# One stored copy of the second block's features, split into parts in the gating-value stage

## The reference, cut to what matters

```python
h = rms_norm(x, pre_norm_w)
proj = h @ w_in                       # 1024 x 7168
hy_in, hy_gate, sg_u, sg_v, sg_gate = jnp.split(proj, [...], axis=-1)
vf = sg_v.astype(jnp.float32).reshape(B, L, N_HEADS_B, HEAD_DIM_B)   # 8 heads of 128
mu = jnp.mean(vf, axis=-1, keepdims=True)
var = jnp.mean(jnp.square(vf - mu), axis=-1, keepdims=True)
vn = (vf - mu) * lax.rsqrt(var + EPS) ...                            # the gating values
```

## Time and profile before

| | |
|---|---|
| median of 3 runs | 3382.54 us (3378.78 to 3385.64) |
| the profiled execution | 3384.93 us, its span 3383.1 us |
| mean granted clock of TensorE | 0.966 of full speed |
| PE busy | 3130.7 us (93%) |
| DVE busy | 2474.3 us (73%) |
| ACT busy | 784.7 us (23%) |
| POOL busy | 296.9 us (9%) |
| DMA | 404.76 MB, mean 120 GB/s |

### The profile page before, as it was taken

One profiled execution on the slowest core, in us unless ns is written; L12 is line 12 of the kernel. 1 busy time (PEld: TensorE's weight loads), 2 busy tenths in 40 slices (PEclk: granted clock), 3 DMA queues, 4 the chain that ended last, 5 costly groups with the idle time before them and its releaser, 6 DMA issues. The chain is left out here.

```text
span 3383.1 us, 32779 instructions
## 1 busy us (share of the span) xinstructions
PE 3130.7 (93%) x12882; PEld 2193.2 (65%) x12882; DVE 2474.3 (73%) x2632; ACT 784.7 (23%) x1354; POOL 296.9 (9%) x420
## 2 busy tenths in 40 slices
PE   6999999888995898999999999999898989889999
PEld 4444445554443687787788888787565656677887
DVE  6989997795883585999999999975556667552221
ACT  2000000683331221000011111112352725431110
POOL 3221220001220350000000000000000000000000
PEclk9999999999997899999999999999999999979999
DMA  6555550202447543665644454421211120334221
GB/s 199 143 141 151 142 154 15 106 1 91 159 155 259 202 131 112 177 167 151 178 139 137 133 145 135 143 75 38 106 53 50 53 100 13 137 111 143 91 91 56
DMA packets 210474, 404.76 MB, mean 120 GB/s; under 512 B 20608, under 2 KB 132416, under 8 KB 202512
## 3 DMA queue, kind: packets, MB, share of 16 engines
q1 hardware_dynamic: 190416, 331.86, 31.4%
q0 software_dynamic: 18752, 62.42, 7.2%
q10 hardware_dynamic: 1152, 8.39, 0.6%
HBM read 316.60 MB, written 86.00 MB: 119 GB/s over the span
## 5 line engine op out<-in xcount | busy, mean ns | idle before, releaser
L1567 PE MATMUL PS<-HH,WH 128*128 128x512 f32 x1536 | 607.6, 396 | 34.6 <-DVE WL L1464 15.4
L1568 PE MATMUL PS<-HL,WH 128*128 128x512 f32 x1536 | 604.6, 394 | 0.0
L1569 PE MATMUL PS<-HH,WL 128*128 128x512 f32 x1536 | 601.8, 392 | 0.0
L741 PE MATMUL PS<-M 128*128 128x512 f32 x1152 | 499.7, 596 | 9.5 <-DVE M L578 7.0
L741 PEld LDWEIGHTS PS<-M 128*128 128x128 f32 x1152 | 219.6, 191 | 289.0 <-issue 278.8
L1567 PEld LDWEIGHTS PS<-HH,WH 128*128 128x128 f32 x1536 | 290.2, 189 | 104.6 <-DVE MB L1501 14.1
L1569 PEld LDWEIGHTS PS<-HH,WL 128*128 128x128 f32 x1536 | 290.2, 189 | 65.3
L1568 PEld LDWEIGHTS PS<-HL,WH 128*128 128x128 f32 x1536 | 290.5, 189 | 61.0
L100 DVE SCALAR_TENSOR_TENSOR HP<-MF,HP 128x1024 f32<-128x1024 f32 x252 | 323.4, 1283 | 8.0
L813 PE MATMUL PS<-M 128*128 128x512 f32 x512 | 224.1, 596 | 5.4 <-DMA M<-pt_scratch 5.4
L2296 PE MATMUL PS<-WH,YH 128*128 128x512 f32 x512 | 201.8, 394 | 14.4 <-DVE WL L2267 9.2
(11 more groups left out here) (210 smaller groups left out, 4695.3 us busy)
## 6 DMA issues: line engine op xcount, KB each, us to landing
MF<-h_scratch SPq DMA_DIRECT2D x380, 256.0 KB, 4.3
M<-c_feat POOLq DMA_DIRECT2D x194, 256.0 KB, 4.3
MF<-w_in SPq DMA_DIRECT2D x56, 512.0 KB, 4.7
M<-u_scratch SPq DMA_DIRECT2D x16, 1024.0 KB, 4.8
M<-w_in SPq DMA_DIRECT2D x18, 512.0 KB, 5.1
M<-x SPq DMA_DIRECT2D x16, 512.0 KB, 5.0
x_scratch<-M SPq DMA_DIRECT2D x16, 512.0 KB, 2.6
h2h_scratch<-HTH SPq DMA_DIRECT2D x16, 512.0 KB, 2.6
```

The costliest lines, as they stand in the source:

```text
L741: ins = t.matmul(PS[:, banks + c, :], wt[:, k], HT[:, k, TC * c:TC * c + TC], start=(k == 0), stop=(k == KD - 1))
L1567: t.matmul(dst, wh, hh, start=(k == 0), stop=False)
L1568: t.matmul(dst, wh, hl, start=False, stop=False)
L1569: ins = t.matmul(dst, wl, hh, start=False, stop=(k == KD - 1))
```

## The change

The first block keeps its features whole: `HTH`, `HTL`, the two splitting operations and one of the two stores are gone. The gating-value stage loads the whole features into `HL` (the tile's place for the low part), ACT rounds them into `HH`, and DVE subtracts in place. The splitting of tiles 0 to 3 goes with that of the four weight quarters; that of tile s + 4 stands at the head of step s, for s up to 11. PE takes the first four tiles of each half quarter by quarter, and the weights of the second half are split two quarters in step 15 and two in step 16, each when step 15's matmuls on the old quarter are done. SP loads only eight tiles ahead of its first store and one in each of the first eight steps.

```diff
@@ first block, ACT and SP
-            def features_high(i):
-                s.wait_ge(h2_done, i + 1)
-                if i >= 2:
-                    s.wait_ge(ht_stored[i % 2], 32 * (i // 2))
-                s.activation(HTH[:, i % 2], HT2[:, i % 2], ACT.Copy).then_inc(hth_done, 1)
-                    sp.wait_ge(htl_done, i - 1)
-                    sp.dma_start(h2h_d[i - 2], HTH[...]).then_inc(ht_stored[i % 2], 16)
-                    sp.dma_start(h2l_d[i - 2], HTL[...]).then_inc(ht_stored[i % 2], 16)
+                    sp.wait_ge(h2_done, i - 1)
+                    sp.dma_start(h2_d[i - 2], HT2[...]).then_inc(ht_stored[i % 2], 16)
@@ first block, DVE
-            def features_low(i):
-                v.wait_ge(hth_done, i + 1)
-                v.tensor_tensor(HTL[:, i % 2], HT2[:, i % 2], HTH[:, i % 2].bitcast(F32), ALU.subtract)...
+            def features_out(i):
+                if i >= 2:
+                    v.wait_ge(ht_stored[i % 2], 16 * (i // 2))
+                ht_evac(i, hs_transposed, G2, HT2[:, i % 2], h2_done)
-                    ht_evac(i - 1, hs_transposed, G2, HT2[:, (i - 1) % 2], h2_done)
-                first_layer_work(2)
-                if i:
-                    features_low(i - 1)
-                first_layer_work(5 if i < 7 else 4)
+                    features_out(i - 1)
+                first_layer_work(7 if i < 7 else 6)
@@ gating values, SP
                 def tokens(i):
-                    sp.dma_start(HH[:, i]..., h2h_d[i]).then_inc(hh_in[i % 4], 16)
-                    sp.dma_start(HL[:, i]..., h2l_d[i]).then_inc(hh_in[i % 4], 16)
+                    if i >= 4:
+                        sp.wait_ge(hh_in[i % 4], 16 * (i // 4))
+                    sp.dma_start(HL[:, i]..., h2_d[i]).then_inc(hh_in[i % 4], 16)
                 values_load(0)
+                tokens(0)
                 values_load(1)
-                tokens(0)
-                values_load(2)
-                values_load(3)
                 tokens(1)
+                for i in (2, 3):
+                    values_load(i)
+                    tokens(i)
 ...
-                for i in range(2, 4):
-                    tokens(i)
                 (three bias loads)
+                for i in range(4, 8):
+                    tokens(i)
                 for r in range(4):
                     row_load(sp, r)
-                for i in range(4, NT):
-                    sp.wait_ge(hh_in[i % 4], 32 * (i // 4))
-                    tokens(i)
                 values_load(4)
                 values_load(5)
                 for s in range(STEPS):
-                    if s == NT:
+                    if s == NT - 1:
                         values_load(6)
                         values_load(7)
+                    if s + 8 < NT:
+                        tokens(s + 8)
                     sp.wait_ge(vn_done, 4 * s + 4)
@@ gating values, ACT
                     if c >= 4:
-                        s_.wait_ge(sv_done, NT)
+                        s_.wait_ge(quarter_done, q + 1)
                     s_.activation(WVH[...], WR[:, c % 2], ACT.Copy).then_inc(wh_done, 1)
+                def features_high(i):
+                    s_.wait_ge(hh_in[i % 4], 16 * (i // 4 + 1))
+                    s_.activation(HH[:, i], HL[:, i].bitcast(F32), ACT.Copy).then_inc(high_done, 1)
                 for c in range(4):
                     values_high(c)
+                    features_high(c)
                 for s in range(STEPS):
-                    if s == NT:
-                        for c in range(4, 8):
-                            values_high(c)
+                    if s + 4 < NT:
+                        features_high(s + 4)
+                    if s in (NT - 1, NT):
+                        values_high(4 + 2 * (s - NT + 1))
+                        values_high(5 + 2 * (s - NT + 1))
                     s_.wait_ge(nb_done, s + 1)
@@ gating values, DVE
+                def features_low(i):
+                    v.wait_ge(high_done, i + 1)
+                    v.tensor_tensor(HL[:, i], HL[:, i].bitcast(F32), HH[:, i].bitcast(F32), ALU.subtract).then_inc(low_done, 1)
                 for c in range(4):
                     values_low(c)
+                    features_low(c)
                 for s in range(STEPS):
 ...
-                    if s == NT:
-                        for c in range(4, 8):
-                            values_low(c)
+                    if s + 4 < NT:
+                        features_low(s + 4)
+                    if s in (NT - 1, NT):
+                        values_low(4 + 2 * (s - NT + 1))
+                        values_low(5 + 2 * (s - NT + 1))
                     v.wait_ge(sv_done, s + 1)
@@ gating values, PE
+                def quarter(s, q):
+                    half, i = s // NT, s % NT
+                    if q == 0:
+                        if s >= 6:
+                            t.wait_ge(vn_done, 4 * (s - 5))
+                        if half == 0:
+                            t.wait_ge(low_done, i + 1)
+                    if i < 4:
+                        t.wait_ge(wl_done, 4 * half + q + 1)
+                    (six matmuls, k = 2 * q and 2 * q + 1, as before)
+                    if s == NT - 1:
+                        ins.then_inc(quarter_done, 1)
+                def four_values(s):
+                    for q in range(4):
+                        for i in range(4):
+                            ins = quarter(s + i, q)
+                            if q == 3:
+                                ins.then_inc(sv_done, 1)
+                four_values(0)
                 (steps 4 and 5, the bias matmuls, steps 6 to 15 as before)
+                four_values(NT)
+                for s in range(NT + 4, STEPS):
                     values(s)
```

More of the change, by code:

```diff
@@ L123, in filter_op, with first_block @@
         link(v.tensor_tensor(acc, total, miss, ALU.add))
-def first_block(nc, A, M, HTH, HTL, PS, x1_d, h1_d, h2h_d, h2l_d):
+def first_block(nc, A, M, PS, x1_d, h1_d, h2_d):
     with ExitStack() as ctx:
@@ L280, in first_block @@
         h2_done = sem("h2_done")
-        hth_done = sem("hth_done")
-        htl_done = sem("htl_done")
         ht_stored = [sem("ht_stored%d" % i) for i in range(2)]
@@ L368, in _ @@
                 if i >= 2:
-                    sp.wait_ge(htl_done, i - 1)
-                    sp.dma_start(h2h_d[i - 2], HTH[:, i % 2].rearrange("p k t -> p (k t)").bitcast(F32)).then_inc(ht_stored[i % 2], 16)
-                    sp.dma_start(h2l_d[i - 2], HTL[:, i % 2].rearrange("p k t -> p (k t)").bitcast(F32)).then_inc(ht_stored[i % 2], 16)
+                    sp.wait_ge(h2_done, i - 1)
+                    sp.dma_start(h2_d[i - 2], HT2[:, i % 2].rearrange("p k t -> p (k t)")).then_inc(ht_stored[i % 2], 16)
             for b in range(2):
                 sp.wait_ge(x1_stored[b], 16 * NT // 2)
-                sp.wait_ge(ht_stored[b], 32 * NT // 2)
+                sp.wait_ge(ht_stored[b], 16 * NT // 2)
             sp.wait_ge(h1_stored, 32)
@@ L676, in _ @@
                     v.sem_inc(h1_done, 1)
-            ht_evac(NT - 1, hs_transposed, G2, HT2[:, (NT - 1) % 2], h2_done)
-            features_low(NT - 1)
+            features_out(NT - 1)
         @block.tensor
@@ L1040, in first_layer, with second_inputs @@
     return count[0]
-def second_inputs(nc, A, PS, behind, CC, HP, kept, h1_d, h2h_d, h2l_d, vn_d, bi_d, u_d, gx_d, yb_d):
+def second_inputs(nc, A, PS, behind, CC, HP, kept, h1_d, h2_d, vn_d, bi_d, u_d, gx_d, yb_d):
     with ExitStack() as outer:
@@ L1139, in second_inputs @@
             hh_in = [stage_sem("hh_in%d" % i) for i in range(4)]
+            high_done = stage_sem("high_done")
+            low_done = stage_sem("low_done")
             sv_done = stage_sem("sv_done")
+            quarter_done = stage_sem("quarter_done")
             stats_done = stage_sem("stats_done")
@@ L1296, in _ @@
             def _(t):
-                def values(s):
+                def quarter(s, q):
                     half, i = s // NT, s % NT
[L1299 to L1305, removed]
+                    if q == 0:
[5 more added lines that the diff above has]
+                        t.wait_ge(wl_done, 4 * half + q + 1)
+                    dst = PS[:, s % 6, :]
+                    for k in (2 * q, 2 * q + 1):
                         hh, hl, wh, wl = HH[:, i, k], HL[:, i, k], WVH[:, k], WVL[:, k]
-                        dst = PS[:, s % 6, :]
                         t.matmul(dst, hh, wh, start=(k == 0), stop=False)
@@ L1310, in values @@
                         ins = t.matmul(dst, hh, wl, start=False, stop=(k == KD - 1))
-                    ins.then_inc(sv_done, 1)
-                for s in range(6):
+                    if s == NT - 1:
+                        ins.then_inc(quarter_done, 1)
+                    return ins
+                def values(s):
+                    for q in range(4):
+                        ins = quarter(s, q)
+                    if s == NT - 1:
```

(27 more changed lines are left out.)

7 lines of the change are left out of this document (1 added, 6 removed).

## The result

| | before | after |
|---|---|---|
| median | 3383.36 us (12 runs) | 3389.09 us (12 runs, 3383.85 to 3393.05) |
| the profiled execution | 3384.93, span 3383.1 | 3392.96, span 3391.1 |
| DMA | 404.76 MB | 387.98 MB |

The ratio is 1.0018, 95% interval 1.0010 to 1.0026: 3.4 to 8.8 us slower. The DMA engines moved 16.8 MB less, and the kernel takes 5.7 us more.

A forecast was written before the change was run, and what follows sets the result against it. It took a closed wait between ACT, DVE and POOL, 6.53 us a step against PE's 5.60, to bound the changed stage: +10.1 us there, -2.4 at the first block's exit, +7.7 in all, median 3390.2 us, range 3382 to 3397.

The forecast's parts named there:

- statistics of step 0: Gating-value stage: DVE's statistics start about 32.1 us after the first issue, 2.5 earlier or 3.5 later possible.
- `NB` 0 to 7, seven rings: Gating-value stage, early steps: seven steps of 6.53 us each, 45.7 us.
- `NB` 7 to 11, with filter: Gating-value stage, steps 8 to 11: filter operations lengthen each step to 8.86 us, four making 35.4.
- The ring: Gating-value steps: rounding waits behind the previous step's normalising, subtraction precedes statistics; 6.53 us a step against PE's 5.60.
- The stage's start: Gating-value stage: PE starts at 7.85 us, step 0 ends at 32.0, statistics start at about 32.1.
- Tile 3's quarter: Gating-value stage's start: tile 3 ready by 18.0 us, its six matmuls take 1.40 us at full clock, ending at 19.4.
- The restart at the half switch: Gating-value stage, change to the second half's weights: PE restarts at the low clock, costing 2.45 us.
- One sign: Gating-value stage: the prediction is wrong if PE waits under 10 us in all between steps 4 and 16.
- The exit: End of the first block: earlier filter store 1.14 us and fewer bytes 1.24 us, together -2.4, between -1.1 and -3.8.
- PE setting the pace: Rival, gating-value stage: splitting costs nothing, PE limits at 5.6 us a step, 3352 us; chance 0.09, whole or by half.
- The kinder ends: Rival: tile 3 ready 2.0 us earlier, exit saves 3.8; 3386.8 us; 0.33 including part of the forecast's spread.
- The low clock in the first four tiles: Rival, gating-value stage: PE slows there, or tile 4 lands late; +2.45 to +5, 3393 to 3395 us; 0.58 with forecast.

The follow-up runs named there:

- the second: The changed kernel run again on one chip with the kernel before: 3390.65 us against 3383.08, ratio 1.0022.
- The two experiments that open the ring: Changed kernel with DVE's subtraction moved behind statistics and filter operations, 3360.67 us; changed kernel with ACT rounding tile s + 5 in step s, 3363.63 us.
- The two-store run: Changed kernel with a second 512 KB store per tile in the first block: 12.9 us from last scaling to the stage's first issue, against 11.7.
- the last experiments: On the changed kernel with DVE's subtraction moved: second half's weights split one step earlier, 3361.18 us; then also both groups of four tiles finished in turn, 3355.75 us.
- the early switch: Changed kernel with DVE's subtraction moved, plus the second half's weights split in steps 14 and 15, not 15 and 16: 3361.18 us, repeated 3359.51.
- the tiles in turn: The early switch kernel with both groups of four tiles finished one after the other after their first quarters: 3355.75 us, repeated 3354.62.
- that kernel with the loads staged: Kernel before, with SP loading only tiles 0 to 7 ahead of its first store and tile s + 8 in step s: 3374.03 us against 3384.71.
- the run with the old half switch: Changed kernel with the second half's weights split in step 16 after all of step 15, tiles 16 to 19 one by one: 3392.51 us against 3384.71.

## Why the prediction was right

**Sign and size.** Forecast +7.7 us; measured +5.7 in the first comparison (interval 3.4 to 8.8) and +7.6 in the second (4.1 to 10.5). The forecast put 0.58 on slower by over 0.2%. The first ratio, 1.0018, lies just short of that bound, the second, 1.0022, just beyond it. At this size the side is chance.

**The steps of the sum**, t in us:

| step | foreseen | measured |
|---|---|---|
| PE starts | 7.85 | 7.56 |
| statistics of step 0 | 32.1 | 34.5 |
| to `NB` of step 0 | 2.7 | 2.7 |
| `NB` 0 to 7, seven rings | 45.7 | 45.8 |
| `NB` 7 to 11, with filter | 35.4 | 35.1 |
| `NB` 11 to 14 | 15.4 | 15.4 |
| to PE's restart | 4.0 | 4.05 |
| to the statistics of step 16 | 20.8 | 20.3 |
| to `NB` of step 31 | 82.0 | 82.1 |
| `NB` of step 31 | 238.1 | 239.9 |

The ring was right to a tenth in steps 1 to 7, because each of its links had a row in the old trace; that a rounding behind a normalising starts 1.38 us after it, for instance, stood there in the half switch. The two experiments that open the ring show that it is the mechanism and not only the number.

Two terms were mis-sized. The stage's start came 2.4 us late. Tile 3's quarter began at t = 18.7 rather than 18.0, and it began at the low clock, after an idle time of 3.13 us, where I had taken full clock: its first eight matmuls took 3.43 us, 1.6 more than at 0.233 each. The restart at the half switch was 0.6 us too dear in the sum: the 2.45 us came from a restart with eleven matmuls at the low clock, and this one had nine and cost 1.9.

The sum's 32.1 for the statistics of step 0 is not far from what the same order gives elsewhere. Nine profiles have the changed kernel's order in the first four tiles, and they give 31.2 to 34.5: 31.2 to 31.6 in the three in which PE kept full clock behind its first restart, 33.0 to 34.5 in the six in which it fell back once. So this term was uncertain by 3 us, as the prediction's bounds had it, and the first profile stands at its late end.

The Trainium skill, "TensorE: Matmul & The Clock Gate", Part 1, says that the throttled state is the default and that activity releases it; by it the prediction would have stood 2.45 us higher. The trace agrees for the gap of 3.13 us, at 1.6 us; behind the gap of 1.43 us just before, PE went on at full clock.

One sign that the prediction named as speaking against it was badly set. It said "wrong" if PE waited under 10 us in all between steps 4 and 16. PE's waits before steps 5 to 15 are 0.72, 0.76, 2.53, 3.01 and 1.78, in all 8.80 us; only with the 16.83 at the half switch are they above 10. The forecast of three waits of about 3 us would have been below 10 as well. The intervals of `NB` decide instead: 6.5 us, not 5.6.

**The exit.** Foreseen -2.4. From the first token store of the loop to the stage's first issue it took 240.5 us before and 238.2 after (1044.60 - 806.43): -2.4. The two-store run confirms the 1.2 us for the bytes. So the stage's +11.9 and the exit's -2.4 make +9.5 in the two profiles, and the spans differ by 8.0. The missing 1.5 us lies in what the sum put at nothing: from PE's first matmul of the next stage to the end the changed kernel took 2099.3 us, the kernel before 2100.9. That +7.7 came so close to these 8.0 is in part luck.

**The rivals.** PE setting the pace fell: that asks for an open ring, and opening it, in two ways, gave 3361 and 3364 us (the prediction had 3352 for it; DVE's own work in steps 8 to 14 and the half switch were still in the way, as the last experiments showed by removing part of it). The kinder ends did not come in this profile. The reason given against them does not hold, though: the first four weight loads landed 4.3 us after their issue (median), the first four feature loads, of the same size, 5.6. The low clock in the first four tiles did come, in one of the gaps.

**What stays open.** The last stages, from PE's first matmul after the switch of stages to the end, took 2098.9 to 2102.2 us over the fourteen profiles; the cause of these 3 us is open. Open is also why the run with two stores had full clock after a gap of 3.14 us and not after one of 2.55.

## What to carry to other kernels

When work is put ahead of an existing chain, write down for each engine what stands in front of it in that engine's own order: a short copy placed behind an operation that waits for another engine can close a ring, and then every step pays the sum of all links although no engine is busy. Here 2.3 us of new work per tile came with a stage 12 us longer than before in one order, and 24 to 26 us shorter in another (with the early switch and the tiles in turn); the better order of the loads is in both. And follow a removed wait to the next one: PE's idle time for loads became idle time for the parts made from them.

## What the runs showed of the hardware that was not expected

**A 5 us difference between executions, far from the change.** At about 175 us DVE waits for a store of the pooling output (view of the waits, DVE, 155 to 205 us; total, times, longest). First the kernel before, then that kernel with the loads staged:

```profile
DVE M L556 <- DMA pt_scratch<-M: 8.8, 1, 8.8
```

```profile
DVE M L556 <- DMA pt_scratch<-M: 3.7, 1, 3.7
```

Over fourteen profiles this wait is 7.3 to 8.8 us in seven and 2.7 to 3.8 in the other seven, in both versions of the first block, and the stage's first issue moves with it: in the kernels with the changed first block and one store 1043.5 to 1044.9 in the first group, 1039.2 to 1040.1 in the second. So two profiles can differ by 5 us ahead of the stage, and t was used above for this reason. Medians of five runs can differ from the stage's own length in the same way; for the runs without a profile this is not shown. What lets the store land late I did not test.

**Idle times and the low clock of TensorE.** Read by the first matmul behind each idle time of PE in this stage (0.47 to 0.50 us at full clock, 0.71 to 0.80 at the low one), the fourteen profiles show this: forty idle times of 0.30 to 2.18 us were followed by full clock, all those of 3.63 us and more by the low one. Those between went both ways: low after 2.36, 2.55, 2.64, 2.75, 2.86, 3.00 (in two profiles), 3.01, 3.13 and 3.17 us, full after 2.53 (in three profiles), 2.84 and 3.14.

The first matmul is not the whole of it. Behind five of the forty (1.78 in two profiles, 1.79, 1.89 and 2.18 us), and behind that of 2.84, the clock fell one to six matmuls later, and then about eight matmuls went at the low clock. So it was in the changed kernel before step 15, where the matmuls start 0.23 us apart, then 0.43, then 0.23 again:

```profile
1158.43 0.39 PE L1314 MATMUL PS<-WVL,HH 128*128 128x512 f32 x1
1158.66 0.56 PE L1312 MATMUL PS<-WVH,HH 128*128 128x512 f32 x1
1159.02 0.63 PE L1313 MATMUL PS<-WVH,HL 128*128 128x512 f32 x1
1159.45 0.63 PE L1314 MATMUL PS<-WVL,HH 128*128 128x512 f32 x1
...
1162.01 0.47 PE L1314 MATMUL PS<-WVL,HH 128*128 128x512 f32 x1
1162.31 0.40 PE L1312 MATMUL PS<-WVH,HH 128*128 128x512 f32 x1
```

A gap of 1.75 us at the same place in the run with the old half switch was followed by full clock throughout. The length of one idle time alone does not decide it here.
